# First scan step's Gram products, masks and solve at the end of attention; context softmax divided on ScalarE; semaphores cleared beside other work

## The reference, cut to what matters

```python
def one(qblk):
    s = jnp.einsum('bkgqd,bksd->bkgqs', qblk, k).astype(jnp.float32) * scale
    p = jax.nn.softmax(s, axis=-1).astype(v.dtype)
    return jnp.einsum('bkgqs,bksd->bkgqd', p, v)
...
def step(S, inp):
    r_t, w_t, k_t, v_t, kk_t, b_t = inp
    sa = jnp.einsum('bhvk,bhk->bhv', S, kk_t)
    S = S * w_t[:, :, None, :] - sa[..., None] * b_t[:, :, None, :] + v_t[..., None] * k_t[:, :, None, :]
    return S, jnp.einsum('bhvk,bhk->bhv', S, r_t)
```

## Time and profile before

| | |
|---|---|
| median of three runs | 921.59 us (920.38 to 922.08) |
| profiled execution | 921.05 us, its span 919.2 us |
| TensorE busy | 844.4 us (92%) |
| VectorE busy | 431.4 us (47%) |
| ScalarE busy | 250.9 us (27%) |
| GpSimd busy | 77.8 us (8%) |
| attention's last VectorE instruction | ends at 360.0 us |
| first work of the scan's block | 362.0 us |
| first work behind the scan's block | about 512.4 us |

### The profile page before, as it was taken

How to read it: one execution, slowest core, us unless ns; L and a number is a source line. 1 busy time by engine, 2 the same in 40 slices (tenths; PEclk the granted TensorE clock), 3 DMA queues, 4 the chain that set the end, 5 groups by cost and what they waited for, 6 DMA issues and landing times. The chain is left out here.

```text
span 919.2 us, 18953 instructions
## 1 busy us (share of the span) xinstructions
PE 844.4 (92%) x8190; PEld 484.8 (53%) x8190; DVE 431.4 (47%) x877; ACT 250.9 (27%) x489; POOL 77.8 (8%) x126
## 2 busy tenths in 40 slices
PE   4999999999989987799988899928999999999997
PEld 3456555544556765788878545514344444333433
DVE  4321466223457886778885765661331000002248
ACT  5002221322588772323322302111111111111110
POOL 1170000000000002122221000120000000000040
PEclk9999999999999996899999899967999999999999
DMA  9999999573990001001322664289989999999993
GB/s 343 323 256 408 379 391 356 202 274 99 344 365 13 14 13 36 5 15 49 96 61 60 206 230 183 84 344 391 377 303 399 408 384 371 418 392 421 418 355 129
DMA packets 72613, 227.89 MB, mean 248 GB/s; under 512 B 10709, under 2 KB 15885, under 8 KB 66129
## 3 DMA queue, kind: packets, MB, share of 16 engines
q1 hardware_dynamic: 60784, 200.33, 58.5%
q10 hardware_dynamic: 7632, 14.64, 4.4%
q0 software_dynamic: 4112, 11.70, 3.8%
HBM read 166.98 MB, written 59.67 MB: 247 GB/s over the span
## 5 line engine op out<-in xcount | busy, mean ns | idle before, releaser
L2581 PE MATMUL ps<-arena 128*32 128x512 f32 (+2 forms) x800 | 170.3, 597 | 1.5 <-ACT arena L2716 1.5
L2581 PEld LDWEIGHTS ps<-arena 128*32 128x32 f32 (+2 forms) x800 | 61.3, 136 | 101.9 <-issue 99.2
L1007 PE MATMUL ps<-arena 128*128 128x128 f32 (+1 forms) x384 | 106.8, 435 | 0.0
L1007 PEld LDWEIGHTS ps<-arena 128*128 128x128 f32 x384 | 58.4, 190 | 50.6 <-issue 48.8
L2138 PE MATMUL ps<-arena 128*128 128x512 f32 x160 | 71.1, 595 | 2.0 <-PEq L1511 2.0
L2623 PE MATMUL ps<-arena 128*32 128x512 f32 (+2 forms) x352 | 70.6, 594 | 0.0
L743 DVE SCALAR_TENSOR_TENSOR arena<-arena 128x128 f32<-128x128 f32 (+3 forms) x56 | 30.9, 552 | 70.2 <-ACT arena L651 68.7
L2892 DVE TENSOR_TENSOR arena<-arena,ps 128x512 f32<-128x512 f32 x12 | 8.3, 688 | 100.2 <-ACT arena L2712 100.2
L886 PE MATMUL ps<-arena 128*128 128x512 f32 (+1 forms) x160 | 52.4, 486 | 0.0
L2138 PEld LDWEIGHTS ps<-arena 128*128 128x128 f32 x160 | 29.5, 190 | 35.6 <-issue 35.6
L2623 PEld LDWEIGHTS ps<-arena 128*32 128x32 f32 (+2 forms) x352 | 24.4, 132 | 38.7 <-issue 37.9
(11 more groups left out here) (392 smaller groups left out, 1314.8 us busy)
## 6 DMA issues: line engine op xcount, KB each, us to landing
gathered_tokens<-arena SPq DMA_DIRECT2D x16, 2560.0 KB, 21.1
arena<-in_exp_up_dram SPq DMA_DIRECT2D x16, 2048.0 KB, 19.8
arena<-in_exp_gate_dram SPq DMA_DIRECT2D x16, 2048.0 KB, 20.6
arena<-in_exp_down_dram SPq DMA_DIRECT2D x16, 2048.0 KB, 22.3
arena<-in_w_mod_dram SPq DMA_DIRECT2D x12, 2048.0 KB, 15.0
arena<-in_w_in_dram SPq DMA_DIRECT2D x4, 2048.0 KB, 12.8
expert_outputs<-arena ACTq DMA_DIRECT2D x10, 512.0 KB, 11.9
arena<-in_x_sample_dram SPq DMA_DIRECT2D x8, 512.0 KB, 9.3
```

The lines of the kernel that those rows point to most:

```text
L1007: mm = pe.matmul(ps[:, b, 0:hi - lo], ring_of(what)[:, k, (e % 4) * P:(e % 4) * P + P], hT[:, k, lo:hi], start=(k == 0), stop=(k == KT - 1))
L2581: mm = pe.matmul(ps[c:c + m, b, :], xgT[:, k, c:c + m], w[n % 3][:, k, :], start=(k == 0), stop=(k == KT - 1))
```

## The change

- `gram(0, 0)` and `gram(0, 1)` move from the head of the scan's block on TensorE to the end of attention, between `values(14)` and the context's transposes; they wait for `first_out`.
- `masked(0, 0)` and `masked(0, 1)` move with them into VectorE's stream of the attention block, between pieces of the solve.
- The solve's rows 13 to 15 move ahead of the block end: all rows are now done in the attention block.
- The context's probabilities are divided by eight ScalarE activations of 128 x 128 with a scale per partition, instead of one VectorE multiplication.
- The clearing block goes. The semaphores of the first phases are cleared by GpSimd during attention, those of attention by GpSimd at step 6 of the scan.
- The tiles of the scan are laid out ahead of the attention block; the addresses stay.

```diff
@@ GpSimd, attention block
                 pool.wait_ge(ld_mask, 16)
+                pool.wait_ge(pv_mm, 6)
+                pool.wait_ge(exp_ok, 12)
+                pool.wait_ge(ev_ok, 5)
+                pool.wait_ge(z_done, 16 * (NE + 2))
+                nc.clear_and_free_semaphores(first_sems)
@@ TensorE, attention block, behind the loop over the pairs
+                pe.wait_ge(first_out, 2)
+                gram(pe, 0, 0)
+                gram(pe, 0, 1)
                 pe.wait_ge(cnorm_ok, 1)
                 pe.wait_ge(pt_ok, 2 * NP2)
@@ ScalarE, attention block
                 ctx_exps(1)
+                act.wait_ge(cinv_ok, 1)
+                for g in range(2):
+                    for j in range(4):
+                        m = 32 + 4 * g + j
+                        ins = act.activation(prob_c[:, g, j], prob_c[:, g, j], ACT.Copy, scale=rinv[:, m:m + 1])
+                ins.then_inc(cnorm_ok, 1)
                 act.wait_ge(ct_mm, 1)
@@ VectorE, attention block
-                ch(dve.reciprocal(rinv[:, 32:40], rsum[:, 32:40]))
-                dve.tensor_tensor(prob_c.rearrange("p g j t -> p (g j) t"), prob_c.rearrange("p g j t -> p (g j) t"),
-                                  rinv[:, 32:40].unsqueeze(2).to_broadcast([P, 8, P]), ALU.mult).then_inc(cnorm_ok, 1)
+                dve.reciprocal(rinv[:, 32:40], rsum[:, 32:40]).then_inc(cinv_ok, 1)
                 divided(NP2 - 2)
-                solve(dve, ch, 1, 11)
+                solve(dve, ch, 1, 4)
+                dve.wait_ge(ld_mask, 16)
+                masked(dve, 0, 0)
+                solve(dve, ch, 4, 7)
+                masked(dve, 0, 1)
+                solve(dve, ch, 7, 11)
                 divided(NP2 - 1)
-                solve(dve, ch, 11, EARLY)
-
-        with nc.Block() as block:
-            @block.gpsimd
-            def _(pool):
-                nc.clear_and_free_semaphores(phase_sems)
+                solve(dve, ch, 11, 16)
@@ GpSimd, scan block
+                    if s == 6:
+                        pool.wait_ge(xt_ok, 3)
+                        pool.wait_ge(solved, 1)
+                        pool.wait_ge(ld_g1, 64)
+                        nc.clear_and_free_semaphores(second_sems)
@@ TensorE, scan block
-                gram(0, 0)
-                gram(0, 1)
                 turn_kb(0)
                 pe.wait_ge(ld_state, 64)
@@ VectorE, scan block
-                solve(dve, ch, EARLY, 14)
-                masked(0, 0)
-                solve(dve, ch, 14, 16)
-                masked(0, 1)
                 turn_back(0, 0)
```

More of the change, by code:

```diff
@@ L390, in place_of @@
             return 5 - k if side_of(z, j) and k >= B_ else k
+        first_sems = list(phase_sems)
         z_again = sem("zrow_set")
@@ L495, in weighted_keys, with place_tile @@
             dve.scalar_tensor_tensor(t_rk[c4 % 2], rws[:, c4, :], rkv[:, c4:c4 + 1], rws[:, 4 + c4, :], ALU.mult, ALU.mult).then_inc(rk_ok, 1)
+        YACC = CHM + 8 * NC4 * T
+        yacc = view(YACC, NCH, NC4, C)
+        ytok = view(YACC, NTT, NHEAD, C)
+        zones = [[SOLVE_END, CB + 12 * T], [CB + NET * T + NCH * NC4 * C, R], [R, CHM],
+                 [YACC + NCH * NC4 * C, 53000], [LORA_AT, LORA_AT + 4 * D_RWKV]]
+        def place_tile(*shape):
+            n = int(np.prod(shape))
+            for zone in zones:
+                if zone[0] + n <= zone[1]:
+                    zone[0] += n
+                    return view(zone[0] - n, *shape)
+            raise AssertionError((n, zones))
@@ new lines, in build @@
+        G = [place_tile(2, 2 * NC4, 2 * C) for _ in range(2)]
+        KB = [place_tile(2, NC4, P) for _ in range(2)]
+        UV = [place_tile(2, NHEAD, C) for _ in range(2)]
+        Mxs = [Mx, view(YACC + 3 * NHEAD * C, 32, 32), Mx]
+        T1, T2 = [place_tile(32, 32) for _ in range(2)], [place_tile(32, 32) for _ in range(2)]
+        states = [place_tile(2, NC4, P) for _ in range(2)]
+        states.append(T2[1].rearrange("q a b -> q (a b)").rearrange("q (z j n) -> q z j n", z=2, j=NC4))
@@ new lines, in build, with both @@
+        stage_in = T1[1].rearrange("q a b -> q (a b)")[:, 0:2 * NC4 * C].rearrange("q (z j n) -> q z j n", z=2, j=NC4)
+        RHc, U1 = place_tile(NHEAD, C), place_tile(NHEAD, C)
+        stage_out = place_tile(2, NC4, C)
+        XTf = [place_tile(NHEAD, 32) for _ in range(2)]
+        Zc = place_tile(NHEAD, 32)
+        pcm = place_tile(2, NC4, NCH, 2)
+        def both(v, z, s, j, first):
+            return v[:, z, chunk_at(z, s), j, first:first + 2, :].rearrange("q k n -> q (k n)")
+        g_mm, g_ok = [[nc.alloc_semaphore(f"{n}_{d}") for d in ("fwd", "bwd")] for n in ("gram_mm", "gram_ok")]
@@ new lines, in gram, with masked @@
+        def gram(pe, s, z):
+            for j in range(NC4):
+                for p in range(2):
+                    mm = pe.matmul(ps[:, 2 * z + p, j * P:(j + 1) * P], both(rows(chm, p), z, s, j, B_), both(rows(chm, p), z, s, j, A_),
+                                   start=True, stop=True)
+            mm.then_inc(g_mm[z], 1)
+        def masked(dve, s, z):
+            dve.wait_ge(g_mm[z], s + 1)
+            dve.tensor_tensor(G[s % 2][:, z].rearrange("q (i y) n -> q i (y n)", y=2),
+                              ps[:, 2 * z:2 * z + 2, :].rearrange("q b (x n) -> q (b x) n", x=2),
+                              mask_s[:, z].rearrange("q y n -> q (y n)").unsqueeze(1).to_broadcast([P, NC4, 4 * C]), ALU.mult).then_inc(g_ok[z], 1)
@@ L1413, in place_tile @@
[L1413 to L1431, removed]
@@ L1432, in build @@
[L1432 to L1433 removed]
+                solve(dve, ch, 1, 4)
[4 more added lines that the diff above has]
+                solve(dve, ch, 7, 11)
+                divided(NP2 - 1)
+                solve(dve, ch, 11, 16)
+        second_sems = phase_sems[len(first_sems):]
         def sems(*names):
             return [[sem(f"{n}_{d}") for d in ("fwd", "bwd")] for n in names]
[L1438 to L1439 removed]
+        t_mm, kb_ok, u_ok, sn_mm, s_add, s_ok, y_ok = sems(
+            "turn_kb", "kb_ok", "u_ok", "sn_mm", "s_add", "s_ok", "y_ok")
@@ L1473, in channels @@
             return chm[:, z, chunk_at(z, s), j, place_of(z, k, j), :]
-        def both(v, z, s, j, first):
-            return v[:, z, chunk_at(z, s), j, first:first + 2, :].rearrange("q k n -> q (k n)")
         def pair_of(v, j):
@@ L1568, in _ @@
             def _(pe):
[L1569 to L1574, removed]
                 def turn_kb(s):
@@ L1717, in _ @@
                             pe.wait_ge(so_ok, 1)
-                        gram(s + 1, 0)
+                        gram(pe, s + 1, 0)
                     pe.wait_ge(xt_ok, s + 1)
@@ L1722, in _ @@
                     if more:
-                        gram(s + 1, 1)
+                        gram(pe, s + 1, 1)
                     cross(s)
@@ L1818, in turn_back @@
                         dve.transpose(T2[g % 2].rearrange("p c m -> p (c m)"), flat).then_inc(solved, 1)
[L1820 to L1824, removed]
                 def z_out(s):
@@ L1858, in _ @@
                     if more:
-                        masked(s + 1, 0)
-                        masked(s + 1, 1)
+                        masked(dve, s + 1, 0)
+                        masked(dve, s + 1, 1)
                     dve.wait_ge(l5_mm, s + 1)
```

7 lines of the change are left out of this document (1 added, 6 removed).

## The result

The changed kernel takes 924.42 us (median of 22 runs, 920.91 to 928.04) against 921.4 us (22 runs, 918.18 to 925.96). The ratio is 1.0040, 95% interval 1.0028 to 1.0051, so +3.7 us (+2.6 to +4.7): slower, and more than the 0.2% that can be told from no change. The two medians themselves lie 3.0 us apart, inside that interval. Single executions of either kernel spread over 7 to 8 us, so a profile's own time proves little here.

A forecast was written before the change was run, and what follows sets the result against it. VectorE's solve was taken to set attention's end, then TensorE the pace of the scan's head. +3.8 us (exposed load) and +0.25 (clock) made +4.05 on 921.05, plus 0.54 for the median: 925.6 us, range 922.5 to 928.0.

The forecast's parts named there:

- VectorE's whole solve before the barrier: End of attention: VectorE's added solve rows and masks delay the scan block's first work from 362.01 to 366.85, +4.85 us.
- The barrier alone: Between attention and scan: 0.55 us from VectorE's end to the scan block's first work.
- The clearing block's 1.45 us: Between attention and scan: without the clearing block, first work would come some 1.45 us sooner.
- The exposed load: Head of the scan block: TensorE waits for the state loads, landing 4.6 us after first work; state products +3.8 us.
- TensorE's clock: Head of the scan block: the 32 state products run at the low clock, 0 to 0.5 us more, taken as 0.25.
- The context path: End of attention: ScalarE divides in at most 3.0 us; last values end 1.0 us before VectorE asks for them.
- fetch hidden by the wait: Head of the scan: code fetched during TensorE's load wait removes the 1.99 us stall, giving 923.6; rival, chance 0.12.
- VectorE was the bound: At `inner(0)`: VectorE's transposes of the solve held it, so it comes 2.8 us sooner, 918.8; rival, chance 0.07.
- clock, +2: First scan step: TensorE stays at the slower clock into it, some +2 us, giving 927.6; rival, chance 0.09.
- absorbed: Behind the scan's head: a later transfer or wait not tied to the scan takes the shift, 921.6; rival, chance 0.06.
- same: Whole kernel: time not told apart from the kernel before, where about 0.2%, 1.8 us, can be told; chance 0.11.
- faster: Whole kernel: time below the kernel before by more than can be told apart, about 0.2%; chance 0.08.

The follow-up runs named there:

- second profile of the changed kernel: The changed kernel itself, nothing altered, run again beside the kernel with only the clearing moved: 923.16 us, ratio 1.0032 to the kernel before.
- the rebalanced kernel: Changed kernel with state loads issued in attention, solve rows 11 to 15 behind the block end, last attention division two rows earlier: 915.71 us, ratio 0.9958.
- the filler: Changed kernel with loads issued in attention, rows 13 to 15 behind the block end, plus 5 unread TensorE products before the block end: 914.97 us, ratio 0.9943.

## Why the prediction was right

It gave 925.6 us, 922.5 to 928.0, and 0.81 for slower; the median is 924.42 and the shift 3.7 us (3.0 between the medians) against my 4.05. The mechanism held; that the sum came so close is in part luck, since two of its terms were off in opposite directions.

- **VectorE's whole solve before the barrier, +4.85 us at first work: right, 0.9 us too large.** First work came at 18.38 us from `values(14)`; the sum put it at 19.27. 0.6 us of the 0.9 lie ahead of `masked(0, 0)`, which did not wait for its Gram records: it started at 351.96 and these had begun at 350.26 with the clock already up (32 records in 2.06 us, not 3.79). 0.2 us is row 13, 1.3 us and not 1.5. In the second profile of the changed kernel the Grams took 2.91 us, the mask waited 0.52, and first work came at 18.82: that wait was priced rightly in kind, and its size changes from run to run.
- **The barrier alone, 0.55 us: right** (365.76 to 366.31). The clearing block's 1.45 us: 1.50 when it was removed alone.
- **The exposed load, 4.6 us from first work: right** (370.85 - 366.26 = 4.59). It is the step that most of the forecast hung on, and issuing the load earlier gave 2.7 us back. The rule of the Trainium skill, page "DMA: Bandwidth & Descriptors", section "Rules for kernel authors" (issue early, wait late), agrees with this run.
- **TensorE's clock, 0.25 us: mis-sized.** The states took 1.97 us and not 1.26, the diagonal records 1.78 and not 1.55: 0.71 + 0.23. So the forecast's 3.8 + 0.25 = 4.05 was 22.92 - 20.09 = 2.83 at the states' start, and 2.83 + 0.94 = 3.77 at `inner(0)`: one term 1 us too large, the other 0.7 too small. That is the luck in it; in the second profile the same two come to 3.22 and 0.96.
- **The context path has 1 us to spare: right and too careful.** ScalarE's eight divisions took 2.45 us and TensorE waited 0.87 us for them, since the Grams were done at 352.3, not 353.8: "before the Grams do" was wrong. `values(15)` still ended at 354.21 + 1.32 = 355.53, 3.4 us ahead of the division that needs it.
- **Rival "fetch hidden by the wait": fell.** TensorE waited 2.60 us for the load and the first stall was 2.01 us all the same. It holds in another place only: when TensorE waits behind a fetch that has already begun, as for `solved` in the rebalanced kernel. The Trainium skill, page "Runtime: NRT & Kernel Launch", section "Instruction fetch mechanics", has the fetch hidden behind slow issue; for 128 pairs of small products in 1.6 us the traces disagree.
- **Rival "VectorE was the bound": fell for these two kernels.** `solved` came 3.3 us sooner and `inner(0)` 3.8 later. With the load gone and the block end early TensorE was still the later one, by 0.7 us (`inner(0)` at 370.41, `solved` at 369.73). VectorE took over only with the filler (1.84 us of waiting for it) or with two more rows behind the block end (3.12).
- **Rivals "clock, +2" and "absorbed": fell.** The part of the clock at the head was 0.9 us; behind it the shift was still 3.8 us at rhs 0, and the time grew by about as much.
- **Readings.** In the earlier trace rows the two lone slices begin at 369.5 and 373.5 us, not 369.0 and 373.0: the code came 2.5 us before TensorE went on, not 3. By the chances given, same adds up to 0.12 and faster to 0.07, not 0.11 and 0.08. Neither changes the forecast.

## What to carry to other kernels

Work that is moved ahead of a barrier delays everything behind it by its own length if its engine is the last to arrive there: three rows of a solve, which VectorE could do behind the barrier with 3 us to spare, cost 4.6 us at `inner(0)` when done ahead of it. Before work is taken from the head of a block, look what it covered: here it was a load of 4.6 us, and issuing that load a block earlier cost nothing. And try the parts of a bundled change apart: the clearing alone made the kernel 0.4 to 0.5% faster, the bundle 0.3 to 0.4% slower.

## What the runs showed of the hardware

- TensorE's code arrives in pieces of 128 pairs of weight load and product; with fast small products the next piece was up to 2.4 us late, and 6, 10, 16 or 22 added records bring the stall just as many records earlier. No piece came between 352 and 374 us, though TensorE was idle for 9.8 us of them.
- Ten filler records in TensorE's idle time ahead of a block end had the next 40 records run at 2.4 GHz (granted clock 1.00) instead of 1.2 (0.50 and 0.56): 1.06 + 1.15 us for 1.94 + 1.83. Six did the same in the rebalanced kernel.
- The same program's scan, from `inner(0)` to the projection, took 141.1 us in one profile and 139.0 in another; 1.6 us of that are two stalls of 0.87 and 0.76 us that only one has. A shift of 4 us in it can only be read against a mark close by.
